# Softmax sums added later, rotations and weight halves taken earlier, and tiles handed over two behind between two layers of a hybrid attention kernel

## The chip, the cores and the metric

One NeuronCore of a Trainium2 chip runs the whole kernel. The metric is the device time of one execution in microseconds (us), the median over the runs. PE is TensorE, ACT ScalarE, DVE VectorE, POOL GpSimd, SP SyncE, which here only issues transfers.

## The reference

Two layers run over 512 latent and 256 context tokens of width 1024. Each has three groups of heads that share one input and one output projection; the last layer needs no context output:

```python
h = layer_norm(x) * (1 + sc) + sh                 # sh, sc, gt from silu(c) @ w_ada + b_ada
gq, gk, gv, dq, dk, dv, mq, mkv, mkr, ga, gb, gc = split(h @ w_in)
o_a = attention(rope(rms(gq)), rope(rms(gk)), gv)            # grouped queries, 6 heads of 64
o_b = rms(attention(q1, k1, dv) - lam * attention(q2, k2, dv))   # differential, 4 heads, q/k of 32
o_c = attention([q_nope, rope(q_pe)], [k_nope, rope(k_pe)], v)   # latent, 6 heads of 64 + 32
y = concat(o_a*silu(ga), o_b*silu(gb), o_c*silu(gc)) @ w_out
x = layer_norm(alpha * x + gt * y) * ln_g + ln_b
```

## The kernel before

Everything is float32. A weight or an activation is split into a rounded half ("high", ACT) and the rest ("low", DVE or POOL), and three matmuls make one product (lines 931 to 933, `three`). The order of every engine is written out by hand, one block per engine, and semaphores tie them together; nothing is scheduled by a tool. `L` is 0 for the first and 1 for the last layer.

**Attention** (`attend` on each engine) goes over ten pairs of maps, p = 0 to 9. Pairs 0, 1, 5 and 6 are differential (one matmul per block of scores), 2 to 4 grouped (two), 7 to 9 latent (three). For pair p PE does these things, and in between the same for its neighbours:

- `max_tile(L, p + 1, i)`, i = 0 to 7 (8 in layer 0): 96 or 128 rows of scores of a coming pair, two banks each, in two places by turns. DVE takes the row maximum (`reduce_max`, L2066), and only then may the tile after the next use the banks.
- `scores(L, p, step)` (L1166), into a ring of three banks; ACT exponentiates each (`exponent`, L1533). A bank is free for the third use behind it when ACT has read it. `RING` lists that order.
- `mix(L, p, step)` (L1182, L1188): probabilities times values, two maps side by side, each 64 columns wide. The "ctx" step is that of the context's own queries, layer 0 only.
- `denominators(L, p)` (L1207, L1210): 32 columns wide. They need the sum of the six exponentiated blocks of a map: POOL adds four of them (`sum_probs`, L1839), DVE the last (`sum_last`, L2092). ACT copies them out (`copy_denominators`), PE turns them (L1218) and the output (L1200), each into the ring.

The latent pairs' operands are made on the way: `mla_head` on PE, `mla_copy` and `mla_high` on ACT (L1425), `mla_rope` (L2074 to L2076) and `mla_low` (L2083, L2085) on DVE. The queries and keys of pairs 5 and 6 are split in `split_block(L, "diff1")` (ACT, then POOL, L1844 and L1847), and SP moves them into place in `load_unit`, with a row of ones for each map.

**Between the layers** PE does the second half of the output projection tile by tile (`project_out`, order 2, 3, 4, 5, 0, 1). DVE adds the residual and normalises a tile (`new_row`), POOL takes the root, ACT writes the next layer's normalised row (`next_row`), PE transposes it (`turn_x`, L965), ACT modulates it (`modulate_next`, L1695), and DVE splits it (`split_next`, L2248, L2249). `LAG = 3` says that tile n - 3 is transposed behind tile n's projection. The next layer's first projection begins with weight slices 0 to 2 for the first two tiles, and then takes slices 3 to 5, which are called HELD: they lie in a place that is free only when the output projection is done, and ACT and POOL split them there.

## Time and profile before

| | |
|---|---|
| time, median of 3 runs | 991.64 us (990.2 to 991.74) |
| the profiled execution's own time | 989.4 us |
| its span | 987.6 us |
| PE busy | 926.8 us (94%) |
| DVE, POOL, ACT busy | 556.1, 509.2, 426.3 us |
| PE waits for DVE's maxima (L1141) | 12.6 us in 10 waits |

A share of busy time says which engine is full, not what a change is worth: for that one looks at what PE waits for and where. Of PE's 61 us of idle time, 21 lie in the first 50 us and 11 in the last 38.

### The profile page before, as it was taken

What the parts mean: (1) busy time and instruction counts of PE and PEld (TensorE: products, weight loads), DVE (VectorE), ACT (ScalarE), POOL (GpSimd) and SP (SyncE); (2) the same over time, 40 slices, a digit from 0 to 9 for tenths busy, and PEclk for the clock granted to TensorE, in tenths of its full rate; (3) what the DMA queues carried; (4) which work ended last, traced back from release to release, by engine and by line L of the source; (5) the groups of instructions that cost most, each with busy time, mean ns of one, the idle gap of its engine ahead of it and who ended that gap; (6) DMA issues with size and microseconds to landing.
All of it is one profiled execution on the core that took longest, in us unless ns stands there. A gap on an engine that the chain in (4) does not pass through costs nothing.

```text
span 987.6 us, 13216 instructions
## 1 busy us (share of the span) xinstructions
PE 926.8 (94%) x4607; PEld 660.9 (67%) x4607; DVE 556.1 (56%) x873; ACT 426.3 (43%) x873; POOL 509.2 (52%) x433
## 2 busy tenths in 40 slices
PE   4799999999989999999999799999997999999996
PEld 1378867789746665666678589888973555565675
DVE  4426525333577569972318847567256757983236
ACT  1512212423546556655334952234343545564432
POOL 2125523324478635566546527455446865566671
PEclk9699999999999999999999999999998999999998
DMA  9955454213522310010253202323351130020242
GB/s 359 333 187 191 146 192 145 64 43 83 139 60 49 82 32 18 17 65 1 98 186 129 94 16 77 93 69 96 79 131 35 33 81 17 17 71 10 99 159 86
DMA packets 44690, 95.88 MB, mean 97 GB/s; under 512 B 9560, under 2 KB 16624, under 8 KB 42576
## 3 DMA queue, kind: packets, MB, share of 16 engines
q1 hardware_dynamic: 44624, 95.03, 31.1%
q8 instruction: 38, 0.62, 0.3%
q14 instruction: 28, 0.23, 0.1%
HBM read 71.33 MB, written 4.21 MB: 76 GB/s over the span
## 4 chain that ended last, share of the span: by engine, by line
PE 79%; DVE 5%; POOL 4%; ACT 4%; issue 3%; DMA 3%; SPq 2%; ACTq 0%; POOLq 0%; DVEq 0%
PE banks L931 15%; PE banks L933 14%; PE banks L932 14%; PE banks L1166 11%; PE banks L1188 10%; PE banks L1141 5%; PE banks L942 2%; DMA area_g<-in_w_ada_dram 2%; PE banks L1207 1%; PE banks L1200 1%; POOL w_split L1791 1%; POOL w_raw L1839 1%; PE banks L1039 1%; DVE area_b L2218 1%; PE banks L1303 1%
## 5 line engine op out<-in xcount | busy, mean ns | idle before, releaser
L1791 POOL TENSOR_TENSOR w_split<-w_raw,w_split 128x512 fp32r<-128x512 f32 (+4 forms) x121 | 147.3, 1226 | 226.5 <-ACT w_split L1425 226.5
L931 PE MATMUL banks<-w_split,area_a 128*128 128x512 f32 (+3 forms) x606 | 230.9, 381 | 10.6 <-DVE area_a L2249 6.8
L933 PE MATMUL banks<-w_split,area_a 128*128 128x512 f32 (+3 forms) x606 | 223.5, 369 | 0.0
L932 PE MATMUL banks<-w_split,area_a 128*128 128x512 f32 (+3 forms) x606 | 223.2, 368 | 0.0
L2066 DVE TENSOR_REDUCE negmax<-banks 128x1 f32<-128x768 f32 x160 | 150.3, 952 | 71.6 <-PE banks L1141 71.2
L1425 ACT ACTIVATE w_split<-w_raw 128x512 fp32r<-128x512 f32 (+4 forms) x121 | 68.4, 580 | 203.4 <-PE banks L933 197.7
L1533 ACT ACTIVATE area_z<-banks 128x512 f32<-128x512 f32 x196 | 108.6, 597 | 84.1 <-PE banks L1166 81.1
L931 PEld LDWEIGHTS banks<-w_split,area_a 128*128 128x128 f32 x606 | 115.1, 190 | 42.1 <-issue 19.8
L1166 PE MATMUL banks<-area_a 97*128 97x512 f32 (+4 forms) x448 | 130.3, 402 | 4.4 <-ACT area_z L1533 3.2
L933 PEld LDWEIGHTS banks<-w_split,area_a 128*128 128x128 f32 x606 | 115.0, 190 | 16.7
L932 PEld LDWEIGHTS banks<-w_split,area_a 128*128 128x128 f32 x606 | 115.4, 190 | 13.0
L1166 PEld LDWEIGHTS banks<-area_a 97*128 97x128 f32 (+2 forms) x448 | 78.1, 192 | 57.4 <-issue 24.3
L1141 PE MATMUL banks<-area_a 96*128 96x384 f32 (+1 forms) x288 | 78.4, 361 | 15.1 <-DVE negmax L2066 12.6
L1188 PE MATMUL banks<-area_z,vals 128*64 128x512 f32 x360 | 91.4, 612 | 0.0
L1839 POOL TENSOR_TENSOR area_b<-area_b,area_z 128x512 f32<-128x512 f32 x56 | 73.9, 1342 | 19.1 <-ACT area_z L1533 19.1
L1141 PEld LDWEIGHTS banks<-area_a 96*128 96x128 f32 (+1 forms) x288 | 50.6, 194 | 43.1 <-issue 34.8
L2039 DVE COPY area_b<-banks 128x512 f32<-128x512 f32 (+1 forms) x27 | 15.7, 583 | 69.1 <-PE banks L1039 69.1
L1425 ACT ACTIVATE area_b<-banks 128x512 f32<-128x512 f32 (+4 forms) x66 | 32.1, 509 | 47.7 <-PE banks L933 24.4
L1820 POOL TENSOR_TENSOR area_g<-area_g,o_v 128x768 f32<-128x768 f32 (+3 forms) x20 | 26.4, 1319 | 49.7 <-DVE o_v L2118 33.6
L1839 POOL TENSOR_TENSOR w_raw<-w_raw,area_z 128x512 f32<-128x512 f32 x38 | 47.5, 1276 | 7.3 <-ACT area_z L1533 7.3
L1796 POOL TENSOR_TENSOR rstd<-var,half 128x8 f32<-128x8 f32 (+2 forms) x30 | 35.4, 1189 | 20.5 <-DVE var L1945 20.5
L1533 ACT ACTIVATE late_bias<-banks 128x512 f32<-128x512 f32 x64 | 35.5, 596 | 23.3 <-PE banks L1166 22.4
(204 smaller groups left out, 1438.6 us busy)
## 6 DMA issues: line engine op xcount, KB each, us to landing
area_g<-in_w_ada_dram SPq DMA_DIRECT2D x16, 1024.0 KB, 5.5
w_raw<-in_w_in_dram SPq DMA_DIRECT2D x32, 512.0 KB, 3.6
area_g<-in_w_ada_dram SPq DMA_DIRECT2D x16, 512.0 KB, 4.9
w_raw<-in_w_out_dram SPq DMA_DIRECT2D x16, 512.0 KB, 4.5
area_a<-parts SPq DMA_DIRECT2D x72, 96.0 KB
area_a<-parts SPq DMA_DIRECT2D x30, 192.0 KB, 3.6
area_b<-in_x_dram SPq DMA_DIRECT2D x8, 512.0 KB, 9.3
w_raw<-in_w_in_dram SPq DMA_DIRECT2D x8, 352.0 KB, 3.9
```

Source lines behind the costliest of these rows:

```text
L931: nc.tensor.matmul(dst, a[0], b[0], start=first, stop=False)
L932: nc.tensor.matmul(dst, a[0], b[1], start=False, stop=False)
L933: return nc.tensor.matmul(dst, a[1], b[0], start=False, stop=last)
L1141: mm = nc.tensor.matmul(banks[:, b0 + j, 0:384], f[0][0:rows, t * P:(t + 1) * P], f[2][0:rows, j * 384:(j + 1) * 384], start=True, stop=True)
L1166: mm = nc.tensor.matmul(dst[:, at:at + cols.stop - cols.start], f[kf][0:rows, kt * P:(kt + 1) * P], f[qf][0:rows, cols], start=(i == 0), s ...
L1188: mm = nc.tensor.matmul(banks[64 * u:64 * u + 64, 3, :], vals[:, step, value_head(2 * p + u), :], prob(L, p, step, u), start=(step == 0), ...
L1425: return nc.scalar.activation(dst, src, ACT.Copy)
L1533: nc.scalar.activation(prob(L, p, step, u), banks[:, r % NRING, :], ACT.Exp, scale=SCALE[pair_family(p)]).then_inc(p_ready, 1)
L1791: op = nc.gpsimd.tensor_tensor(lo, raw, hi.bitcast(F32), ALU.subtract)
L1796: nc.gpsimd.tensor_tensor(rstd[:, cols], var[:, cols], half[:, cols], ALU.pow).then_inc(root_ready, 1)
L1839: nc.gpsimd.tensor_tensor(total(L, p, u), first, prob(L, p, step, u), ALU.add).then_inc(pool_summed, 1)
L2066: nc.vector.tensor_reduce(negmax[:, p % 2, at:at + 1], banks[:, b0:b0 + 2, 0:384], AX.XY, ALU.max, negate=True).then_inc(max_read, 1)
```

## The change

It moves instructions on PE, ACT, DVE and SP, takes five small transfers per layer away, and moves one split from POOL to DVE. Counts of the arithmetic stay as they are. The diff is cut: first the tables, then SP's loads, PE's `attend` and `project_out`, ACT's `attend` and DVE's `attend`.

```diff
-LAG = 3
+LAG = 2
...
-        return (2, 4, 6, 0, 6, 0)[out_tiles(L - 1).index(use[2])] + use[3]
+        return (2, 4, 6, 4, 0, 6)[out_tiles(L - 1).index(use[2])] + use[3]
...
-LOADS = {"gqa": 3, "diff": 7, "mla": 3}
+ONES = (12, 13, 14)
+def loads(u):
+    own = u < 4 or u in (16, 19)
+    return {"gqa": 3, "diff": 6, "mla": 2}[family(u)] + int(own)
...
+                for b in ONES:
+                    slab_used(sp, L, b - KD)
+                    load_one(blocks[96:97, b, :], ones_in)
...
                     if context:
+                        scores(L, p, 2)
+                        max_tile(L, p + 1, 8)
                         mix(L, p - 1, "ctx")
+                        denominators(L, p - 1)
                     else:
                         mix(L, p - 1, 4)
                         mix(L, p - 1, 5)
-                    scores(L, p, 2)
-                    max_tile(L, p + 1, 8)
-                    denominators(L, p - 1)
+                        denominators(L, p - 1)
+                        scores(L, p, 2)
                     scores(L, p, 3)
...
+                    both = out_tiles(L)[:2] if L == DEPTH - 1 and n == 0 else [t]
...
                     for k in range(KD):
                         pe.wait_ge(w_lo, N_SLICE["out", L, 1, k])
-                        mm = three(bank(use), [h_t[:, i, k, t * P:(t + 1) * P] for i in range(2)],
-                                   late_slice(k), k == 0, k == KD - 1)
+                        for o in both:
+                            mm = three(bank(("y", L, 1, o)), [h_t[:, i, k, o * P:(o + 1) * P] for i in range(2)],
+                                       late_slice(k), k == 0, k == KD - 1)
...
-                    if head_pair(p + 2):
-                        mla_high(L, 2 * p + 4)
                     exponent(L, p, 1)
                     if context:
+                        exponent(L, p, 2)
                         copy_context(L, p - 1)
+                        copy_denominators(L, p - 1)
                     else:
                         copy_latents(L, p - 1)
+                        copy_denominators(L, p - 1)
+                        exponent(L, p, 2)
                     if head_pair(p + 2):
                         mla_high(L, 2 * p + 5)
-                    exponent(L, p, 2)
-                    copy_denominators(L, p - 1)
                     exponent(L, p, 3)
...
+                    if p == 2:
+                        split_block(L, "diff1")
...
                     if context:
                         exponent(L, p, "ctx")
+                    if head_pair(p + 3):
+                        mla_high(L, 2 * p + 6)
...
                 for i in range(EARLY):
                     reduce_max(L, 2, i)
-                    if i in (2, 3):
-                        sum_last(L, 0, i - 2)
...
                     reduce_max(L, p + 1, 6)
-                    if head_pair(p + 2):
-                        mla_low(L, 2 * p + 4)
+                    sum_last(L, p - 1, 0)
+                    sum_last(L, p - 1, 1)
                     reduce_max(L, p + 1, 7)
...
                     reduce_max(L, p + 2, 1)
+                    if head_pair(p + 3):
+                        mla_rope(L, 2 * p + 6)
+                    if p == 2:
+                        split_last(L)
                     reduce_max(L, p + 2, 2)
                     reduce_max(L, p + 2, 3)
                     if head_pair(p + 3):
-                        mla_rope(L, 2 * p + 6)
-                    if p < NPAIR:
-                        sum_last(L, p, 0)
+                        mla_rope(L, 2 * p + 7)
                     reduce_max(L, p + 2, 4)
-                    if p < NPAIR:
-                        sum_last(L, p, 1)
                     reduce_max(L, p + 2, 5)
                     if diff:
                         diff_norm(L, p - 1)
                     if head_pair(p + 3):
-                        mla_rope(L, 2 * p + 7)
+                        mla_low(L, 2 * p + 6)
```

`RING` is rewritten to match. `last_pair` is changed in the same way. `split_last` is the low half of "diff1", as two tensor_tensor on DVE, taken off POOL. In the last layer DVE keeps two tiles in work: `gained_tile` of the next tile stands ahead of `new_row` of tiles 0 and 2. ACT calls `next_row` ahead of `modulate_next` for every tile.

**DVE at the start of attention, last layer.** L2066 (L2090 in the changed file) is the row maximum of a tile; the first two and the last of pair 1 and those of pair 2 stand here. L2092 (L2125) is the last addition of pair 0, into `w_raw`. Before:

```order
L2066 TENSOR_REDUCE negmax<-banks 128x1 [waits filled,max_filled]
L2066 TENSOR_REDUCE negmax<-banks 128x1 [waits max_filled] x2
L2092 TENSOR_TENSOR w_raw<-w_raw,late_bias 128x512 [waits p_ready,pool_summed]
L2066 TENSOR_REDUCE negmax<-banks 128x1 [waits max_filled]
L2092 TENSOR_TENSOR w_raw<-w_raw,late_bias 128x512 [waits p_ready,pool_summed]
L2066 TENSOR_REDUCE negmax<-banks 128x1 [waits max_filled] x4
L2106 RECIPROCAL rec<-banks 128x8 [waits ring_filled]
```

The same place of the changed kernel:

```order
L2090 TENSOR_REDUCE negmax<-banks 128x1 [waits filled,max_filled]
L2090 TENSOR_REDUCE negmax<-banks 128x1 [waits max_filled] x6
L2125 TENSOR_TENSOR w_raw<-w_raw,late_bias 128x512 [waits p_ready,pool_summed] x2
L2090 TENSOR_REDUCE negmax<-banks 128x1 [waits max_filled]
L2139 RECIPROCAL rec<-banks 128x8 [waits ring_filled]
```

Both additions moved behind four more maxima, with one left behind them.

**PE in pair 5, last layer.** From the last `mix` of pair 4 (L1188, L1198 in the changed file) over the denominators (L1207, L1217), scores 2 and 3 of pair 5 (L1166, L1176) and a maximum tile of pair 7 (L1141, L1151) to the transposed output (L1200, L1210). Before:

```order
L1188 MATMUL banks<-late_bias,vals 64x512
L1166 MATMUL banks<-area_a 128x512 [waits p_ready] x2
L1207 MATMUL banks<-area_b,ones_c 32x512 [waits p_ready,dve_summed]
L1207 MATMUL banks<-area_b,ones_c 32x512
L1166 MATMUL banks<-area_a 128x512 [waits p_ready] x2
L1141 MATMUL banks<-area_a 128x384 [waits max_read,mla_lo,unit_in14]
L1141 MATMUL banks<-area_a 128x384
L1218 MATMUL banks<-ident,scr 128x64 [waits d_copied]
L1218 MATMUL banks<-ident,scr 128x64 x3
L1200 MATMUL banks<-ident,o_t 128x128 [waits p_ready,o_copied]
```

The same place of the changed kernel:

```order
L1198 MATMUL banks<-late_bias,vals 64x512
L1217 MATMUL banks<-area_b,ones_c 32x512 [waits p_ready,dve_summed]
L1217 MATMUL banks<-area_b,ones_c 32x512
L1176 MATMUL banks<-area_a 128x512 [waits p_ready] x2
L1176 MATMUL banks<-area_a 128x512 [waits d_copied]
L1176 MATMUL banks<-area_a 128x512 [waits p_ready]
L1151 MATMUL banks<-area_a 128x384 [waits mla_lo,max_read,ones_in,unit_in14]
L1151 MATMUL banks<-area_a 128x384
L1228 MATMUL banks<-ident,scr 128x64 [waits p_ready,d_copied]
L1228 MATMUL banks<-ident,scr 128x64 x3
L1210 MATMUL banks<-ident,o_t 128x128 [waits p_ready,o_copied]
```

The denominators moved ahead of scores 2, and one bank of scores 3 now waits for their copy (`d_copied`).

**ACT at the same place.** L1533 (L1554) are exponentials, L1425 (L1446) copies: `area_a<-area_b` is `mla_high`, `o_t` the output of pair 4, `scr` its denominators. Before:

```order
L1425 ACTIVATE area_b<-banks 64x256 [waits ring_filled]
L1533 ACTIVATE area_z<-banks 128x512 [waits pool_summed,p_used,ring_filled] x2
L1425 ACTIVATE area_a<-area_b 96x512 [waits ring_filled,mla_roped]
L1425 ACTIVATE area_a<-area_b 64x768
L1533 ACTIVATE area_z<-banks 128x512 [waits pool_summed,p_used,ring_filled] x2
L1425 ACTIVATE o_t<-banks 128x512 [waits p_used,ring_filled]
L1425 ACTIVATE area_a<-area_b 96x512 [waits ring_filled,mla_roped]
L1425 ACTIVATE area_a<-area_b 64x768
L1533 ACTIVATE area_z<-banks 128x512 [waits pool_summed,p_used,ring_filled] x2
L1425 ACTIVATE scr<-banks 64x512 [waits ring_filled,rec_done]
L1533 ACTIVATE late_bias<-banks 128x512 [waits dve_summed,p_used,ring_filled] x2
```

The same place of the changed kernel:

```order
L1446 ACTIVATE area_b<-banks 64x256 [waits ring_filled]
L1446 ACTIVATE area_a<-area_b 96x512 [waits ring_filled,mla_roped]
L1446 ACTIVATE area_a<-area_b 64x768
L1554 ACTIVATE area_z<-banks 128x512 [waits pool_summed,p_used,ring_filled] x4
L1446 ACTIVATE o_t<-banks 128x512 [waits p_used,ring_filled]
L1446 ACTIVATE scr<-banks 64x512 [waits ring_filled,rec_done]
L1554 ACTIVATE area_z<-banks 128x512 [waits pool_summed,p_used,ring_filled] x2
L1446 ACTIVATE area_a<-area_b 96x512 [waits ring_filled,mla_roped]
L1446 ACTIVATE area_a<-area_b 64x768
L1554 ACTIVATE late_bias<-banks 128x512 [waits dve_summed,p_used,ring_filled] x2
```

One `mla_high` moved ahead of the pair's first exponential, the other from between exponentials 1 and 2 to between 2 and 3.

## Rows read from the trace of the kernel before

**Rows 1.** The page, part 1: busy time, share of the span, instructions.

```profile
PE 926.8 (94%) x4607; PEld 660.9 (67%) x4607; DVE 556.1 (56%) x873; ACT 426.3 (43%) x873; POOL 509.2 (52%) x433
```

**Rows 2.** PE's waits: for whom, us in total, times, longest.

```profile
PE banks L1141 <- DVE negmax L2066: 12.6, 10, 5.2
...
PE banks L1141 <- DMA area_a<-ones_r: 1.0, 2, 0.6
```

**Rows 3.** Timeline, attention's start, layer 0: start, duration, instruction [idle before].

```profile
278.25 1.81 POOL L1844 TENSOR_TENSOR parts<-area_b,parts 128x768 fp32r<-128x768 f32 x1
...
277.11 3.51 DVE L2092 TENSOR_TENSOR w_raw<-w_raw,area_z 128x512 f32<-128x512 f32 x1 [0.98 <-POOL w_raw L1839]
...
281.63 0.98 PE L1141 MATMUL banks<-area_a 128*128 128x384 f32 x2 [3.42 <-DVE negmax L2066]
```

**Rows 4.** Timeline, the same place in the last layer, and pair 2's.

```profile
746.53 2.96 DVE L2092 TENSOR_TENSOR w_raw<-w_raw,late_bias 128x512 f32<-128x512 f32 x1 [1.93 <-POOL w_raw L1839]
...
747.66 1.28 POOL L1844 TENSOR_TENSOR parts<-area_b,parts 128x512 fp32r<-128x512 f32 x1
...
750.50 0.98 PE L1141 MATMUL banks<-area_a 128*128 128x384 f32 x2 [5.17 <-DVE negmax L2066]
...
771.28 0.59 PE L1141 MATMUL banks<-area_a 128*128 128x384 f32 x2 [0.93 <-DVE negmax L2066]
```

**Rows 5.** Stretches: busy time of PE, PEld, DVE, ACT, POOL, PE's clock, DMA.

```profile
568.00:571.40 3.40, 3.40 (x8) 2.68 (x9) 2.83 (x4) 1.07 (x3) 1.71 (x2) 0.50 0.14 17
750.50:755.90 5.40, 5.40 (x14) 3.46 (x16) 4.11 (x5) 2.17 (x4) 1.70 (x2) 0.50 0.58 134
772.00:778.00 6.00, 6.00 (x29) 2.85 (x26) 1.41 (x3) 3.36 (x6) 5.63 (x6) 1.00 0.41 94
```

**Rows 6.** Timeline, narrow steps between wide ones.

```profile
445.43 0.40 PE L1135 MATMUL banks<-cmp_t 96*128 96x256 f32 x2
...
445.76 0.62 PE L1207 MATMUL banks<-area_b,ones_c 128*32 128x512 f32 x2
...
446.21 0.60 PE L1207 MATMUL banks<-area_b,ones_c 128*32 128x512 f32 x2
...
446.75 0.97 PE L1166 MATMUL banks<-parts 97*128 97x512 f32 x3
```

**Rows 7.** Timeline, pair 5 of the last layer.

```profile
832.45 1.05 PE L1207 MATMUL banks<-area_b,ones_c 128*32 128x512 f32 x4
834.34 0.98 PE L1166 MATMUL banks<-area_a 97*128 97x512 f32 x2 [0.84 <-ACT area_z L1533]
...
836.00 0.66 PE L1200 MATMUL banks<-ident,o_t 128*128 128x128 f32 x4
...
828.39 1.35 ACT L1425 ACTIVATE area_a<-area_b 96x512 fp32r<-96x512 f32 x2
829.65 1.06 ACT L1533 ACTIVATE area_z<-banks 128x512 f32<-128x512 f32 x2
...
830.37 3.12 POOL L1839 TENSOR_TENSOR area_b<-area_z 128x512 f32<-128x512 f32 x2 [7.37 <-ACT area_z L1533]
```

**Rows 8.** Timeline, the same stretch, DVE.

```profile
827.70 0.68 DVE L2092 TENSOR_TENSOR area_b<-area_b,late_bias 128x512 f32<-128x512 f32 x1
828.30 0.95 DVE L2066 TENSOR_REDUCE negmax<-banks 128x1 f32<-128x768 f32 x1
...
833.97 0.94 DVE L2085 TENSOR_TENSOR area_a<-area_b,area_a 64x768 fp32r<-64x768 f32 x1
```

**Rows 9.** Timeline, between the layers.

```profile
567.84 0.80 PE L931 MATMUL banks<-w_split,area_a 128*128 128x512 f32 x1 [6.80 <-DVE area_a L2249]
...
568.43 1.28 POOL L1791 TENSOR_TENSOR cmp_t<-w_raw,cmp_t 128x512 fp32r<-128x512 f32 x1
```

**Rows 10.** Timeline, end of the program.

```profile
957.33 0.50 PE L931 MATMUL banks<-cmp_t,area_a 128*128 128x512 f32 x1 [0.57 <-POOL cmp_t L1791]
...
983.23 1.28 DVE L2235 SCALAR_TENSOR_TENSOR area_b<-o_t,row_std,area_g 128x1024 f32<-128x1024 f32 x1 [0.97 <-POOL row_std L1804]
```

126 lines of the change are left out of this document (78 added, 48 removed).

## The prediction, made blind

> **What bounds the kernel now.** I read the page, then the waits of PE, then the timeline of all engines where PE waits. PE is busy for 94% of the span [rows 1], so a change that leaves PE's work as it is can give back only what PE waits for, and what it does at the lower of its two clocks. The waits view puts 12.6 us on DVE's row maxima, in ten waits [rows 2]; two of them are most of it. At the start of attention PE is idle for 3.42 us in layer 0 [rows 3] and for 5.17 us in the last layer [rows 4], because DVE stands at `sum_last` and the maxima are queued behind it. Behind that idle time, and behind the 6.80 us between the layers [rows 9], the granted clock is 0.50, that is 1.2 GHz, for 3.4 to 5.4 us; in a stretch without such a wait before it it is 1.00 [rows 5].
>
> The other waits are small and stand at fixed places: in the differential pairs next to the latent ones (5 and 6), where ACT has `mla_high` between the exponentials [rows 7], and at the weights of the last projection [rows 10]. The sum is made against the profiled execution, 989.4 us, which is 2.2 us below the median of the runs, 991.64.
>
> **Attention's start, layer 0.** The DVE add of 277.11 took 3.51 us for what takes 0.68 elsewhere [rows 3, 8]: it ended 0.56 us behind POOL's split, which ran from 278.25 to 280.06. The changed DVE does maxima 3, 4, 5 and 6 of pair 2 first. Max 3's scores were there at 276.5, so the tile that started at 281.63 can start at 277.95. From there I put durations in PE's new order: scores 0 at 278.3, max 6 at 278.8, scores 1 until 279.9, scores 2 until 281.5 (its second bank waits for an exponential), max 8 until 281.95, context mix until 282.95. The two adds now stand behind max 6 on DVE (280.8) and meet POOL's first sum of pair 1, so they end at 283.4 and the denominators start at 283.45. Before, the same set of instructions ended with denominators at 287.4. Gain 4.0 us, the lower clock's part included.
>
> **The same, last layer.** Max 3 can be read at 744.6, so the tile of 750.50 starts at 745.6. Scores 0, max 6, scores 1, max 7 and the two mixes bring PE to 749.75. The denominators now follow at once, and their adds are late: POOL is at sums until 747.7 and at the split until 748.94 [rows 4], then one add, one POOL sum (1.26), one add: 751.4. Denominators until 752.45 and scores 2 until 752.95; scores 3 begin there against 758.65 before, less some 0.3 for the bank that waits for `d_copied`. Gain 5.2 us. Bounds: 3.9 if both of POOL's queued operations pass first, as in the 2.96 us of 746.53 [rows 4], 6.5 if the adds wait for nobody.
>
> **The pairs after it.** The adds no longer stand between maxima 3, 4 and 5. That removes PE's 0.93 us at 771.28 [rows 4] and two of its kind (0.62 at 789.1, 0.3 at 764.7), all three read off the same view as the ten waits of [rows 2]: 1.9 us. Against it, in the last layer's grouped pairs the adds come some 0.2 us later than the mixes end: two matmuls per bank give 4.7 us from scores 0 to the denominators, and DVE needs 4.9 (maximum 6 until 2.35, add, one POOL sum, add). Three pairs, 0.6 us. Net -1.3.
>
> **Rows of ones and "diff1".** PE waits twice for a row of ones, 1.0 us in total [rows 2], 1.3 with the restart. The split is taken before scores 4 of pair 2 instead of behind them, its low half goes to DVE, which then stands without its adds there, and each load has one transfer less. DVE's two subtractions (0.7 and 0.9 [rows 8]) hold up maximum 2, whose successor on PE is due over 2 us later: nothing. Gain 1.3; without that cover a loss of 1.6 per layer.
>
> **Narrow steps side by side.** A 256-column matmul goes out every 0.12 us, but the 32-column one follows the last (445.55) after 0.21: 0.09 to enter [rows 6]. Inside, the pace is 0.45 (445.76 to 446.21), and the wide one comes 0.54 later (446.75): 0.09 to leave. The change removes one leaving and one entering in each of 18 places. No row has 64 columns directly followed by 32. Its cost lies between nothing and one of these 0.09, so a place gives 0.09 to 0.18; I take 0.1, since both kinds of entry cost the same here. In seven places the adds are late anyway (below) and nothing is gained: 11 x 0.1 = 1.1 us. The Trainium skill, TensorEngine Tiling (Array Packing), Key Properties, says that changing the tiling mode, not just the tile, drains the engine; by it 64 to 32 is such a change, which leaves one of two and is the lower value. The trace has no such pair to confirm it.
>
> **Pairs 5 and 6: a loss.** These have one matmul per bank, so PE is fast and ACT and DVE are late. Last layer, pair 5, from scores 0 at 826.99: `mla_low` now stands between maxima 5 and 6. Max 5 ends at 828.65, `mla_low` (0.6 + 0.94 [rows 8]) at 830.1, max 6 (0.9) at 831.0. POOL's two sums of pair 5 begin at 829.3, when the exponential is there, and the add waits for the second: 831.8, so the adds end at 832.4 and 833.1. PE is at the denominators at 831.0 and waits 2.1 us. Then denominators until 834.05, copy on ACT until 834.75, exponential 2 until 835.8, `mla_high` (1.35 [rows 7]) until 837.1, first half of exponential 3 at 837.7. The transposed output needs that bank, in the ring of three: 837.8 instead of 836.00 [rows 7]. Loss 1.8 us, although the old wait of 0.84 at 834.34 is gone. Layer 0 gives the same sum (add ready 1.6 us behind the context mix, output at 376.1 instead of 374.4): 1.7. Two pairs in each layer: +7.0. Bounds: if the adds wait for nobody and DVE is early, the output comes at 835.7, -0.3 each and -1 in all; if each add loses one more POOL sum, +12. I take the chain. Pair 7 of the last layer has the same `mla_low` and a `diff_norm` ahead of max 6, with 5.4 us on PE until the denominators and 7 on DVE: +1.3. Pair 7 of layer 0 has the context's steps as cover.
>
> The Trainium skill, SBUF — State Buffer, Who interferes with whom, calls the pair of ports that DVE and GpSimd share an exclusive lock, for DVE operations with two SBUF inputs too, where the first to issue blocks the other for its whole length. The trace agrees (3.51 against 0.68 us), and it speaks against this change, which puts adds where POOL's sums begin.
>
> **Between the layers.** Before, PE waits from 561.0 for tile 3's split, 6.80 us [rows 9], then runs 3.8 us at the lower clock. With tiles two behind, ACT has per tile two squares (1.34 each), a row (1.25) and a modulation (2.9): 6.8 us, more than PE's 6.3, so PE waits 1.1 and 1.0 us for the first and fourth row. Slices 0 to 2 of tiles 2 and 3 then run from 561.5 to 565.6 unhindered. But now the HELD slices are due: POOL's last split, 568.43 to 569.7 [rows 9] with PE not waiting for it, comes at 570.5 to 571.8, because ACT's second square stands behind the HELD high halves and later than before. PE waits 6.2 us for that and runs on slowly. Slices 6 and 7 begin at 591.9 instead of 591.2: +0.7. What is late next is the weights, no longer the rows. Bounds -3 (the split at 568) and +3.
>
> **The end.** The first tile of the last projection takes 8.9 us instead of 5.5, since its slices 4 to 7 come one each 1.3 to 1.7 us [rows 10]. Two tiles by turns need 1.37 us per slice, so nothing waits: both are done at 964.84, the last tile at 975.8 instead of 979.25. DVE has 4.35 us per tile, four tiles from 964.2, and ends at 981.7 instead of 984.5 [rows 10]. -2.8, bounds -3.4 and -1.5 (two stores back to back).
>
> **Sum.** -4.0 - 5.2 - 1.3 - 1.3 - 1.1 + 7.0 + 1.3 + 0.7 - 2.8 = -6.7 us: 982.7 on the profiled execution's scale, 984.9 on the median's; I say 984.5.
>
> **Rivals.** *The adds are in time* (0.27). DVE reaches them before POOL's first sum, or gets the ports between two sums. For it: POOL is idle for 7.37 us ahead of 830.37 [rows 7]. Against it: DVE's own queue ends at 831.0. Then pairs 5 to 7 give -1 instead of +8.3, and the sum is about -16: 975.5. *The boundary gives what it was laid out for* (0.10): the HELD slices are split by 567 and PE's wait is gone, 6.2 us and the slow clock: 977. *No change* (0.04): the new waits take all of it, because the ring and not the adds bounds pairs 1 to 4 too: 990. *Slower* (0.07): every add waits for one more POOL sum, 1.26 us, in all 18 places. The forecast gain is used up at 0.37 us a pair; at 0.7 (half hidden) it is 12.6 - 6.7, or 997.5. For it: both long adds [rows 3, 4] let two POOL operations pass. Against it: in most pairs POOL has one operation in flight.
>
> **How the numbers follow.** My case has 0.52, with a range of its own of 981 to 989. The range 974 to 989.5 takes in the first two rivals and leaves out the others, about 2 in 10 with the edges. A measurement of this kernel tells from about 0.2%, or 2 us. Faster by more: 0.52 + 0.27 + 0.10, less a little at the upper edge, 0.88; within it 0.05; slower 0.07.
>
> **What would show it.** Right: no idle before the sixth tile of pair 2; the adds of pairs 5 and 6 over 1.2 us each, with PE's wait in front of the denominators put on DVE's add; a wait for ACT ahead of the transposed output; a wait for `cmp_t` from POOL between the layers; no wait in the last projection. Wrong: no wait at the denominators of pairs 5 and 6 (then 975), or one at nearly all pairs (then slower).

## The result: 0.7% slower

The changed kernel takes 998.34 us (median of 4 runs, 997.83 to 998.81), the kernel before 990.92 us on the same chips (4 runs, 989.47 to 991.74): ratio 1.0074, 95% interval 1.0059 to 1.009. The prediction was 984.5 us, with 989.5 as its upper end. The profiled execution took 998.17 us with a span of 996.4 us, 8.8 us more than the span before.

The page, part 1, of the changed kernel:

```profile
PE 929.0 (93%) x4607; PEld 660.9 (66%) x4607; DVE 567.4 (57%) x877; ACT 427.8 (43%) x873; POOL 510.9 (51%) x429
```

DVE is busy 11 us longer than in [rows 1]. The four subtractions of "diff1" that it took over are 4.8 of them; the rest is the same arithmetic, taking longer. PE's waits (for whom, us in total, times, longest):

```profile
PE banks L1151 <- DVE negmax L2090: 7.0, 9, 2.1
PE banks L1217 <- DVE area_b L2125: 6.1, 6, 3.0
PE banks L944 <- POOL cmp_t L1815: 5.6, 1, 5.6
PE banks L1217 <- DVE w_raw L2125: 4.4, 5, 2.8
PE banks L1210 <- ACT area_z L1554: 4.1, 4, 1.3
...
PE banks L1210 <- ACT late_bias L1554: 1.4, 2, 1.1
```

The long waits for maxima of [rows 2] are gone, 12.6 us became 7.0. In their place stand 10.5 us at the denominators (L1217), in eleven waits for DVE's last additions (L2125), and 5.5 us at the transposed output (L1210).

To find the place, I compared the start of the same ACT exponential in both timelines; their order is the same in both kernels.

| exponential | before, us | after, us | difference | gained or lost since the row above |
|---|---|---|---|---|
| layer 0, pair 0, first | 262.58 | 262.56 | -0.02 | |
| pair 1, first | 283.08 | 278.78 | -4.30 | -4.3 |
| pair 5, first | 366.57 | 362.44 | -4.13 | +0.2 |
| pair 7, first | 416.96 | 415.06 | -1.90 | +2.2 |
| pair 8, first | 439.98 | 439.01 | -0.97 | +0.9 |
| pair 9, fourth | 469.31 | 467.95 | -1.36 | -0.4 |
| last layer, pair 0, first | 731.97 | 732.63 | +0.66 | +2.0 |
| pair 1, fourth | 759.32 | 755.91 | -3.41 | -4.1 |
| pair 5, first | 827.42 | 821.66 | -5.76 | -2.4 |
| pair 7, first | 871.25 | 876.30 | +5.05 | **+10.8** |
| pair 8, first | 890.97 | 902.27 | +11.30 | **+6.2** |
| pair 9, fourth | 917.02 | 927.77 | +10.75 | -0.6 |
| end of the span | 987.6 | 996.4 | +8.8 | -2.0 |

So the change did most of what it was to do, and 17 us were lost in three pairs, 5 to 7 of the last layer. The timeline of DVE, PE and POOL in pair 5 there (start, duration, instruction, idle before):

```profile
820.13 0.69 DVE L2098 TENSOR_TENSOR scr<-area_b,rt 32x512 f32<-32x512 f32 x1
...
821.55 0.68 DVE L2100 TENSOR_TENSOR area_b<-area_b,scr 32x512 f32<-32x512 f32 x1
...
822.27 1.82 DVE L2090 TENSOR_REDUCE negmax<-banks 128x1 f32<-128x768 f32 x2
823.37 0.58 PE L1151 MATMUL banks<-area_a 96*128 96x384 f32 x2 [1.51 <-DVE negmax L2090]
...
824.73 0.94 DVE L2109 TENSOR_TENSOR area_a<-area_b,area_a 64x768 fp32r<-64x768 f32 x1
824.96 3.52 POOL L1863 TENSOR_TENSOR area_b<-area_z 128x512 f32<-128x512 f32 x2 [7.26 <-ACT area_z L1554]
...
826.46 2.56 DVE L2125 TENSOR_TENSOR area_b<-area_b,late_bias 128x512 f32<-128x512 f32 x2
...
829.08 1.05 PE L1217 MATMUL banks<-area_b,ones_c 128*32 128x512 f32 x4 [0.85 <-DVE area_b L2125]
...
833.67 0.63 PE L1210 MATMUL banks<-ident,o_t 128*128 128x128 f32 x4 [1.07 <-ACT late_bias L1554]
```

`mla_rope` (2.1 us) now stands ahead of maximum 4, and PE waits 1.51 us for that maximum. Then come `mla_low`, maximum 6, and the additions, which meet POOL's first sums: 2.56 us for two, where two alone take 1.4 [rows 8]. Pairs 6 and 7 repeat it with waits of 2.08 and 1.13 us for the maximum and 0.84 and 3.04 us at the denominators (the expectation of e9 below puts the last in pair 6; it stands in pair 7). None of this came singly: behind the waits the granted clock falls. Stretches of the changed kernel (busy time of PE, PEld, DVE, ACT, POOL, PE's clock, DMA):

```profile
819.00:822.00 3.00, 2.86 (x14) 1.30 (x10) 2.92 (x5) 1.75 (x4) 0.00 (x0) 1.00 0.12 28
...
824.30:827.70 3.40, 3.40 (x11) 1.21 (x10) 3.40 (x5) 1.00 (x2) 2.74 (x2) 0.53 0.00 0
...
834.50:837.90 3.40, 3.40 (x11) 0.77 (x8) 3.40 (x4) 0.27 (x1) 2.70 (x2) 0.53 0.03 6
...
885.70:889.10 3.40, 3.40 (x9) 1.64 (x6) 0.46 (x1) 0.91 (x2) 0.00 (x0) 0.53 0.00 0
```

There are five such rows between 824 and 890 (two more from 851.6 and from 861.8), 17.0 us in which PE is busy without a gap at a mean clock of 0.53, that is mostly at 1.2 GHz. At full clock the same work takes 17.0 x 0.53, so they cost 8.0 us. The kernel before had no such stretch in these pairs. The rest is PE's waits, 11.9 us there against 3.1: with the 8.0 this makes 16.8 of the 17.1 us.

### The profile page after: what moved, and what is told of

It is laid out like the page before. It is cut to its first block, busy times and chain, and to the rows that moved or that the text cites. A ratio compares the mean times of both kernels' runs of the same rounds, so it can differ in the third digit from the quotient of the medians.

```text
span 996.4 us, 13272 instructions
## 1 busy us (share of the span) xinstructions
PE 929.0 (93%) x4607; PEld 660.9 (66%) x4607; DVE 567.4 (57%) x877; ACT 427.8 (43%) x873; POOL 510.9 (51%) x429
## 4 chain that ended last, share of the span: by engine, by line
PE 72%; DVE 15%; ACT 4%; DMA 3%; POOL 3%; issue 2%; SPq 1%; POOLq 0%; ACTq 0%; DVEq 0%
PE banks L944 14%; PE banks L946 13%; PE banks L945 13%; PE banks L1176 9%; PE banks L1198 8%; DVE negmax L2090 4%; PE banks L1151 4%; PE banks L955 2%; PE banks L1217 2%; DMA area_g<-in_w_ada_dram 2%; DVE area_b L2125 2%; DVE w_raw L2125 1%; PE banks L1210 1%; DVE area_b L2099 1%; DVE area_b L2100 1%
## 5 line engine op out<-in xcount | busy, mean ns | idle before, releaser
L2090 DVE TENSOR_REDUCE negmax<-banks 128x1 f32<-128x768 f32 x160 | 148.4, 950 | 62.2 <-PE banks L1151 61.8
L1446 ACT ACTIVATE w_split<-w_raw 128x512 fp32r<-128x512 f32 (+4 forms) x121 | 68.3, 580 | 204.6 <-PE banks L946 198.9
L1554 ACT ACTIVATE area_z<-banks 128x512 f32<-128x512 f32 x196 | 109.1, 599 | 83.4 <-PE banks L1176 72.8
L1176 PE MATMUL banks<-area_a 97*128 97x512 f32 (+4 forms) x448 | 128.0, 399 | 1.2 <-ACT late_bias L1554 0.4
L1176 PEld LDWEIGHTS banks<-area_a 97*128 97x128 f32 (+2 forms) x448 | 78.0, 190 | 47.5 <-issue 23.7
L1198 PE MATMUL banks<-area_z,vals 128*64 128x512 f32 x360 | 94.9, 632 | 0.0
L1151 PE MATMUL banks<-area_a 96*128 96x384 f32 (+1 forms) x288 | 77.1, 356 | 8.5 <-DVE negmax L2090 7.0
L1151 PEld LDWEIGHTS banks<-area_a 96*128 96x128 f32 (+1 forms) x288 | 49.8, 190 | 35.0 <-issue 28.2
L2063 DVE COPY area_b<-banks 128x512 f32<-128x512 f32 (+1 forms) x27 | 15.7, 583 | 69.1 <-PE banks L1049 69.1
L1863 POOL TENSOR_TENSOR w_raw<-w_raw,area_z 128x512 f32<-128x512 f32 x38 | 49.6, 1331 | 8.8 <-ACT area_z L1554 8.6
L1446 ACT ACTIVATE area_b<-banks 128x512 f32<-128x512 f32 (+4 forms) x66 | 32.0, 508 | 50.1 <-PE banks L946 23.8
L1554 ACT ACTIVATE late_bias<-banks 128x512 f32<-128x512 f32 x64 | 35.7, 599 | 22.7 <-PE banks L1176 18.2
```

What stands on the lines that cost most here:

```text
L1151: mm = nc.tensor.matmul(banks[:, b0 + j, 0:384], f[0][0:rows, t * P:(t + 1) * P], f[2][0:rows, j * 384:(j + 1) * 384], start=True, stop=True)
L1176: mm = nc.tensor.matmul(dst[:, at:at + cols.stop - cols.start], f[kf][0:rows, kt * P:(kt + 1) * P], f[qf][0:rows, cols], start=(i == 0), s ...
L1198: mm = nc.tensor.matmul(banks[64 * u:64 * u + 64, 3, :], vals[:, step, value_head(2 * p + u), :], prob(L, p, step, u), start=(step == 0), ...
L1446: return nc.scalar.activation(dst, src, ACT.Copy)
L1554: nc.scalar.activation(prob(L, p, step, u), banks[:, r % NRING, :], ACT.Exp, scale=SCALE[pair_family(p)]).then_inc(p_ready, 1)
L1863: nc.gpsimd.tensor_tensor(total(L, p, u), first, prob(L, p, step, u), ALU.add).then_inc(pool_summed, 1)
```

## Experiments

Fifteen kernels, by the question that each answers. "Both back" means the changed kernel with adds and rotations at their old places. Results first; ratios are to the kernel before on the same chip.

| run | median, us | ratio (95% interval) |
|---|---|---|
| e1: DVE's ropes back | 1009.32 | 1.0177 (1.0154 to 1.02) |
| e2: ropes, `mla_low`, `mla_high` back | 1004.26 | 1.0128 (1.0107 to 1.0149) |
| e3: adds of pairs 1 to 9 back | 1000.51 | 1.0084 (1.006 to 1.0108) |
| e4: both back | 986.25 | 0.9947 (0.9929 to 0.9966) |
| e5: e4, layer 0's second `mla_high` of a pair behind exponential 2 | 984.88 | 0.9962 (0.9939 to 0.9985) |
| e6: e5, between the layers as before | 986.89 | 0.996 (0.9945 to 0.9975) |
| e7: e4, denominators behind scores 2 | 984.84 | 0.9947 (0.9927 to 0.9967) |
| e8: before, only the end changed | 990.33 | 0.9993 (0.998 to 1.0005) |
| e9: changed, POOL waits for the adds | 985.08 | 0.994 (0.9919 to 0.9962) |
| e10: combined | 979.96 | 0.989 (0.9872 to 0.9908) |
| e11: combined, POOL waits in pair 1 | 972.11 | 0.9809 (0.9791 to 0.9826) |
| e12: before, only pair 0's adds late | 983.41 | 0.9922 (0.9894 to 0.9951) |
| e13: e2 and POOL waits | 998.09 | 1.0062 (1.0042 to 1.0082) |
| e14: e3 and POOL waits | 990.91 | 0.9993 (0.9973 to 1.0014) |
| e15: e11 with two tiles behind | 976.33 | 0.9832 (0.9809 to 0.9855) |

### Adds or rotations? e1 to e4

e1, on DVE:

```diff
-                    if head_pair(p + 3):
-                        mla_rope(L, 2 * p + 6)
                     reduce_max(L, p + 2, 2)
                     reduce_max(L, p + 2, 3)
                     if head_pair(p + 3):
-                        mla_rope(L, 2 * p + 7)
+                        mla_rope(L, 2 * p + 6)
                     reduce_max(L, p + 2, 4)
                     reduce_max(L, p + 2, 5)
                     if diff:
                         diff_norm(L, p - 1)
+                    if head_pair(p + 3):
+                        mla_rope(L, 2 * p + 7)
```

> Theory R (rotations): in the changed kernel DVE has a whole mla_rope (2.1 us) ahead of maximum 4, so it is late at the maxima of the latent pairs; in pairs 5 to 7 of the last layer PE waits 4.7 us in three waits for them, and the granted clock is 0.53 for 3.4 us behind each. Only the two mla_rope go back to their old places here. R expects these 4.7 us and three of the five slow stretches (1.7 us each) gone: 998.3 - 9.8 = 988.5 us. Theory A (adds): the loss comes from the last additions, which wait for POOL behind maximum 6; the ropes are not what is late. A expects 996 to 998.5 us, with the 4.7 us turned into waits for the adds.

1009.32 us: neither theory. The waits for maxima on L1151 fell from 7.0 to 2.9 us, and the adds became later still: 15.7 us in four waits at the denominators, the longest 5.2. The second rope now stands behind maximum 5 and ahead of `mla_low`, maximum 6 and the adds: in pair 5 of the last layer DVE goes without a pause from that rope (829.68) to the adds (836.07), and PE waits 5.15 us for them.

e2 puts `mla_low` behind maximum 6 and both `mla_high` behind exponentials 0 and 1 as well.

> As the run before, but mla_low on DVE and mla_high on ACT go back too, so that only the adds and the order of the narrow steps stay changed in attention. R expects 986 to 989 us (the old 0.84 us wait for an exponential behind mla_high comes back, the ones at the transposed output go). A expects 995 to 998 us and the waits at the denominators of pairs 5 and 6 unchanged at 0.9 us or more each.

1004.26 us, 16.5 us in six waits at the denominators. The adds now stand behind maximum 6 and `mla_low`.

e3, the adds:

```diff
                     reduce_max(L, p + 1, 6)
-                    sum_last(L, p - 1, 0)
-                    sum_last(L, p - 1, 1)
+                    if p == 1:
+                        sum_last(L, 0, 0)
+                        sum_last(L, 0, 1)
...
+                    sum_last(L, p, 0)
                     reduce_max(L, p + 2, 4)
+                    sum_last(L, p, 1)
                     reduce_max(L, p + 2, 5)
```

> The changed kernel with the last additions of pairs 1 to 9 back between maxima 3, 4 and 5; pair 0's stay where the change puts them, and the rotations stay changed. A expects the 10.5 us of PE's 11 waits at the denominators gone and two slow stretches of 1.7 us with them: 984.5 us. R expects only the waits outside pairs 5 to 7 gone, since DVE is late at the maxima there all the more: 998.3 - 4.5 = 993.8 us, or worse.

1000.51 us (nine runs from 992.95 to 1003.6, the widest scatter of all). The waits for the adds in pairs 1 to 9 are gone, and PE waits 9.4 us in eleven waits for maxima: adds and ropes stand ahead of them. Pairs 5 to 7 of the last layer lose 17.0 us, as much as in the changed kernel.

> Adds of pairs 1 to 9 and all rotation steps back; changed remain the start of attention, the narrow steps side by side, the ones and diff1, the boundary and the end. By the trace of the two kernels attention lost 3.2 us in pairs 5 to 7 of layer 0 and 17.1 in the last layer, both of which should be gone: 998.3 - 20.3 = 978 us, if R and A between them are the whole loss. If a third thing (denominators directly behind the value steps, with their bank and copy) holds part of it, 982 to 988 us, with PE waiting for ACT's copies in pairs 5 to 7.

e4 holds both edits and takes 986.25 us. Against it the adds' move alone costs 18.0 us (e2), the rotations' alone 14.3 (e3), and the two together 12.1 (the changed kernel). So the costs do not add: they are one queue, DVE's, between maximum 3 and the denominators. The time lies in the expectation's other range, that of a third cause. By the profile (982.76 us, the lowest of six runs) pairs 5 to 7 still lose 3.9 us in layer 0, where PE waits 1.82 us twice for an exponential behind `mla_high`, and 1.8 in the last layer.

### The order of the denominators, the boundary, the end: e5 to e8

```diff
 # e5, ACT, layer 0 only
-                    if head_pair(p + 2):
-                        mla_high(L, 2 * p + 5)
                     if context:
                         exponent(L, p, 2)
                         copy_context(L, p - 1)
                         copy_denominators(L, p - 1)
+                    if head_pair(p + 2):
+                        mla_high(L, 2 * p + 5)
```

> The last kernel (both back, 986.25 us) with one more edit: in layer 0 the second mla_high of a pair stands behind exponential 2, not between 1 and 2. There PE waits 1.82 us twice for an exponential behind mla_high (pairs 5 and 6 of layer 0), and the trace shows a stretch at clock 0.53 behind each. Theory 'the copy on ACT's queue is the whole of what is left in these pairs': 3.6 us of waits and two times 1.7 us of slow clock go, 986.25 - 7 = 979 us. Rival 'the ring only hands the wait on to the transposed output', as in the changed kernel (3 waits of about 1.1 us): 984 to 986 us.

984.88 us, not told from e4 by the intervals. In layer 0, pairs 5 to 7 lose 5.8 us against before (first exponentials of pairs 5 and 8), where e4 lost 3.9. The time is the rival's, but the trace speaks for neither theory, because the edit moved the wrong copy. Both waits of 1.82 us are still there:

```profile
363.15 1.57 ACT L1446 ACTIVATE area_a<-area_b 96x768 fp32r<-96x768 f32 x2
...
365.25 0.54 PE L1176 MATMUL banks<-area_a 97*128 97x512 f32 x1 [1.82 <-ACT area_z L1554]
```

PE waits here for exponential 1, which stands behind the pair's first `mla_high`, and that one e5 leaves in its place. New are waits of 1.31 us twice and 0.43 us once for the transposed output, whose bank waits for exponential 3 behind the copy that was moved.

e6 is e5 with `LAG = 3`, the old bank map, PE's old first slices and ACT's old order.

> The kernel of the run before with the part between the layers put back (LAG = 3, bank map, order of first slices, ACT's order of row and modulation). The milestones put the next layer's first exponential 2.0 us later against the last one of layer 0 in the changed kernel than before, and 3.7 us in the kernel with both back. If two tiles behind is a loss of its own (HELD slices split late), this run is 2.0 to 3.7 us faster than the one before it. If the difference is only where the slow stretch falls against PE's idle time, it is within 1 us of it either way. The prediction's term would make it 0.7 us faster.

986.89 us, unclear: the two scatter by 6 and 9 us. By the profiles, from pair 9's fourth exponential to the next layer's first, three tiles behind are 0.9 us faster. See e15.

e7 is e4 with scores 2 ahead of the denominators again, in `RING`, on PE and on ACT.

> The both-back kernel of the first four runs with the denominators behind scores 2 again (ring, PE and ACT orders of before); left of the change are pair 0's adds, ones and diff1, the boundary and the end. The prediction's term (0.1 us in 11 of 18 places, here in all 18) says 1.1 to 1.8 us slower than with them side by side, if nothing else moves; but the 1.82 us waits in layer 0 and the 0.84 us waits for the denominators' copy in the last layer belong to the order, so those (5.3 us and slow stretches of 1.7 us) go and before's 1.7 us come back. Theory 'the order itself loses': 980 to 983 us. Theory 'the order itself is worth its 1.8 us': 987 to 988 us.

984.84 us, between the two theories and the same as e4, from parts of opposite sign. In pairs 5 to 7 of layer 0 it loses 0.1 us against before, where e4 lost 3.9. In pairs 1 to 4 the side-by-side order of e4 is 0.57 us better in layer 0 and 0.54 us from pair 2 to 5 in the last layer, 0.14 and 0.18 a place. And at the start of the last layer e7 is 3.9 us worse:

```profile
745.61 1.29 POOL L1853 TENSOR_TENSOR w_raw<-w_raw,area_z 128x512 f32<-128x512 f32 x1
746.85 1.28 POOL L1858 TENSOR_TENSOR parts<-area_b,parts 128x512 fp32r<-128x512 f32 x1
747.11 7.07 DVE L2115 TENSOR_TENSOR w_raw<-w_raw,late_bias 128x512 f32<-128x512 f32 x2
748.09 2.50 POOL L1853 TENSOR_TENSOR w_raw<-area_z 128x512 f32<-128x512 f32 x2
750.55 2.48 POOL L1853 TENSOR_TENSOR w_raw<-w_raw,area_z 128x512 f32<-128x512 f32 x2
754.24 1.07 PE L1217 MATMUL banks<-w_raw,ones_c 128*32 128x512 f32 x2 [4.59 <-DVE w_raw L2115]
```

Two additions that take 1.4 us alone took 7.07: the first 6.47, the second 0.68. POOL ran six operations without a pause from 745.61 to 753.03, five of them still to end when the first addition began, and it ended only behind the last of them. With exponential 2 ready early, POOL had two sums more to go on with.

e8 has only the end in the kernel before.

> The kernel before with only the end changed (two tiles of the last projection by turns, DVE with two tiles in work). Prediction's term: -2.8 us, 990.7 - 2.8 = 987.9. Bounds -3.4 and -1.5. Rival 'stores and the last normalisation hold the end whatever PE does': 990.7 within 0.5 us.

990.33 us against 991.05, not told from no change by its interval. By the trace the part behind pair 9's fourth exponential takes 68.65 us instead of 70.58: -1.9 us, and 68.5 to 68.7 in every profile with the changed end.

### POOL against DVE: e9, e13, e14

```diff
             def sum_probs(L, p, step):
                 for u in range(2):
+                    if step == 1 and PN[L, p] >= 1:
+                        pool.wait_ge(dve_summed, N_DVE_SUM[PAIRS[PN[L, p] - 1] + (1,)])
```

> The changed kernel with one wait more: POOL begins a pair's first sum only when DVE's last additions of the pair before are done, so the two never meet there. In the changed kernel these additions take up to 2.3 us each at the start of the last layer (two in 4.65 us, while POOL is busy without a gap), where they take 0.68 alone, and PE waits 10.5 us in 11 waits for them. Theory L (DVE's additions get nothing while POOL goes on): most of the waits at the denominators go (the 2.84 us of pair 0 in the last layer, 3.0 in pair 6), 7 to 9 us with the slow stretches: 988 to 991 us. Theory Q (DVE's own queue of mla_low, maximum 6 and the ropes is late; POOL is not the matter): only pair 0's wait goes, 995 us, and PE's waits in pairs 5 to 7 stay within 1 us of what they are.

985.08 us: one wait more on POOL made the changed kernel 13.3 us faster, more than the 7 to 9 us of theory L. At the start of the last layer, in e9:

```profile
746.09 1.26 POOL L1870 TENSOR_TENSOR parts<-area_b,parts 128x512 fp32r<-128x512 f32 x1
746.32 2.19 DVE L2127 TENSOR_TENSOR w_raw<-w_raw,late_bias 128x512 f32<-128x512 f32 x2
...
748.56 1.05 PE L1217 MATMUL banks<-w_raw,ones_c 128*32 128x512 f32 x4 [0.38 <-DVE w_raw L2127]
...
748.63 2.51 POOL L1865 TENSOR_TENSOR w_raw<-area_z 128x512 f32<-128x512 f32 x2 [1.29 <-DVE w_raw L2127]
```

The same place of the changed kernel:

```profile
748.38 1.28 POOL L1868 TENSOR_TENSOR parts<-area_b,parts 128x512 fp32r<-128x512 f32 x1
748.61 4.65 DVE L2125 TENSOR_TENSOR w_raw<-w_raw,late_bias 128x512 f32<-128x512 f32 x2
...
749.62 2.48 POOL L1863 TENSOR_TENSOR w_raw<-area_z 128x512 f32<-128x512 f32 x2
...
753.31 1.05 PE L1217 MATMUL banks<-w_raw,ones_c 128*32 128x512 f32 x4 [2.84 <-DVE w_raw L2125]
```

The additions take 2.19 us, the rest of POOL's split, and PE's wait falls from 2.84 to 0.38. In all, the denominators' waits fell from 10.5 to 1.5 us, and of the 17.0 us at the lower clock in pairs 5 to 7, 10.2 are left. The 4.7 us of waits for maxima there are unchanged, and these pairs still lose 10.1 us against before, by the first exponentials of pairs 5 and 8. e13 and e14 ask what holds that rest.

e13 is e2 with e9's wait, e14 is e3 with it.

> The changed kernel with POOL's wait and with all rotation steps (mla_rope, mla_low, mla_high) back at their old places; the adds stay behind maximum 6. With POOL's wait alone it took 985.1 us, and pairs 5 to 7 of the last layer still lost 10 us against before, with 4.7 us of PE's waits on row maxima. Theory 'the ropes' new places hold the rest': the 4.7 us and up to two slow stretches go, 977 to 980 us. Theory 'the queue in front of the adds' (mla_low, then maximum 6, then the adds; without POOL's wait this kernel's PE waited 16.5 us in six waits at the denominators): POOL's wait gives back only POOL's part, and the time is 986 to 992 us, slower than with the ropes early.

> The changed kernel with POOL's wait and the adds of pairs 1 to 9 back between maxima 3, 4 and 5; the rotations stay changed. Theory 'ropes': PE's waits on maxima in pairs 5 to 7 of the last layer (6.9 us in four waits with the adds back and no wait on POOL) stay, since the adds there were never late: 988 to 992 us. Theory L alone (POOL and DVE meeting at the adds is the whole loss): 978 to 982 us.

PE's waits in pairs 5 to 7 of the last layer, in e13 and then in e14:

```profile
PE banks L1217 <- DVE area_b L2128: 9.8, 3, 3.4
PE banks L1151 <- DVE negmax L2093: 0.8, 2, 0.4
```

```profile
PE banks L1151 <- DVE negmax L2092: 7.0, 4, 2.7
PE banks L1210 <- ACT late_bias L1554: 1.4, 2, 1.1
PE banks L1210 <- ACT area_z L1554: 1.1, 1, 1.1
```

998.09 and 990.91 us. POOL is out of the way in both, and DVE's own queue is still late: with adds behind `mla_low` and maximum 6 at the denominators (9.8 us), with ropes ahead of maximum 4 at the maxima (7.0 us). Only with both back (e4) are both kinds gone: 2.8 us of waits for maxima in the last layer, none for adds.

### The start alone and the best combination: e10 to e12, e15

e12 is the kernel before with one edit:

```diff
                 for i in range(EARLY):
                     reduce_max(L, 2, i)
-                    if i in (2, 3):
-                        sum_last(L, 0, i - 2)
...
                     reduce_max(L, p + 1, 6)
+                    if p == 1:
+                        sum_last(L, 0, 0)
+                        sum_last(L, 0, 1)
```

> The kernel before with one edit: pair 0's two additions behind maximum 6 of the first iteration instead of between the early maxima, in both layers. The prediction's terms are -4.0 in layer 0 and -5.2 in the last layer: 991 - 9.2 = 981.8 us. In the traces so far the milestones give -4.3 in layer 0 (adds hidden) and, with scores 2 ahead of the denominators as here, -5.5 + 3.9 in the last layer, because POOL goes on without a gap there and DVE's two additions took 7.07 us: 991 - 5.9 = 985.1 us. No gain at all (991) if the clock's slow stretch at both places stays.

983.41 us, -7.3 on its chip and between the two forecasts: two instructions moved give as much as the whole change was forecast to give (-6.7). The profile is that of the fastest run (980.04 us); in it the start gains 4.3 us in layer 0, up to pair 1's first exponential, and 5.9 in the last layer, up to its fourth. The order at the start of the last layer is that of e7, yet the two additions took 2.52 us there, not 7.07, and PE did not wait for them:

```profile
744.32 1.27 POOL L1844 TENSOR_TENSOR parts<-area_b,parts 128x512 fp32r<-128x512 f32 x1
745.30 2.52 DVE L2092 TENSOR_TENSOR w_raw<-w_raw,late_bias 128x512 f32<-128x512 f32 x2
...
745.62 3.34 POOL L1839 TENSOR_TENSOR w_raw<-area_z 128x512 f32<-128x512 f32 x2
```

PE was at 1.2 GHz from 742.5 to 745.9, POOL had a gap of 0.02 us behind its split, and the first addition, begun 0.3 us before the split's end (in e7 1.0 before), was done at 746.14, in the middle of POOL's next sum. So the same order gave 2.5 us in one kernel and 7.1 in the other. That the gap decides it is my reading and not shown.

e10 takes e4, with the old order of scores 2 and denominators in pairs 5 to 7 and the boundary of before:

```diff
+def side(p):
+    return not 5 <= p <= 7
...
+        if not side(_p):
+            RING += row + third + den
+        elif ctx:
+            RING += third + row + den
+        else:
+            RING += row + den + third
```

and the same case on PE and ACT. e11 adds one wait:

```diff
+                    if step == 1 and p == 1:
+                        pool.wait_ge(dve_summed, N_DVE_SUM[PAIRS[PN[L, p] - 1] + (1,)])
```

> What the runs so far speak for: pair 0's adds late, all other adds and the rotations where they were before, denominators side by side with the value steps except in pairs 5 to 7 (there the old order), ones and diff1, the boundary as before, the end as changed. Worked out against the kernel with the denominators back (984.84 us): the boundary of before 1.5 to 2 us faster at the same clock, the narrow steps 0.16 us a place in some 10 places by the milestones, and the start of the last layer 2.5 us less (its adds took 7.07 us there and 2.5 to 4.65 with denominators ahead of scores 2). Sum 984.84 - 6 = 979 us. If these pieces do not add because each moves the place of the next slow stretch: 983 to 986 us.

> The kernel of the run before, with POOL's first sum of pair 1 waiting for DVE's additions of pair 0 in both layers. Theory L: in the last layer these two additions end at 1.4 us instead of 4.65 us behind their start, and PE's wait of 2.84 us in front of the first denominators goes: 2.8 us faster than the run before, 976 us, up to 1.7 us more where a slow stretch goes too. Theory Q: no difference over 0.5 us.

979.96 us, as worked out from the pieces, and 972.11 us, 1.9% faster than the kernel before and 4 us below what theory L gave. The profile of e11 is that of its slowest run, 976.22 us, which is what theory L gave; there the start of the last layer is 2.6 us faster than in e10. The two profiles differ by 3.9 us; the rest of the 7.9 between the medians no trace shows. In e11 the two additions stand so:

```profile
744.11 1.27 POOL L1899 TENSOR_TENSOR parts<-area_b,parts 128x512 fp32r<-128x512 f32 x1
745.23 1.31 DVE L2156 TENSOR_TENSOR w_raw<-w_raw,late_bias 128x512 f32<-128x512 f32 x2
...
747.56 1.05 PE L1227 MATMUL banks<-w_raw,ones_c 128*32 128x512 f32 x4
```

No wait at all in front of the denominators (e10: 2.8 us).

> The fastest kernel so far (combined, POOL waiting in pair 1, 972.11 us) with the change's part between the layers put in. At the same place of the slow stretch the milestones make two tiles behind 1.5 to 2 us slower: 973.6 to 974.1 us, up to 1.7 us more if the stretch moves. The prediction's term of +0.7 gives 972.8; its other bound, -3 (the HELD slices split in time), 969.

976.33 us. The intervals of e15 and e11 just overlap, but the profiles agree: from pair 9's fourth exponential to the next layer's first it takes 262.7 to 264.4 us in six profiles with three tiles behind (mean 263.6) and 264.5 to 266.3 in eleven with two (mean 265.3). The two pairs of kernels that differ in nothing else give less: 0.9 us (e5, e6) and 0.7 (e15, e11).

## Why the prediction was wrong, step by step

**The step that failed: "Pairs 5 and 6: a loss", +7.0, with pair 7's +1.3.** For the last layer it gave 3.6 for two pairs and 1.3 for the third; they cost 10.8 and 6.2. In both layers these pairs cost 20.2 us instead of 8.3, and that is 11.9 of the 15.5 us between the forecast of -6.7 and the 8.8 of the profile.

In layer 0 the size was near, 3.4 forecast and 2.2 measured for pairs 5 and 6 (and 0.9 in pair 7, where nothing was forecast), but that was in part luck. PE waited 0.47 and 0.46 us for the adds there, not 1.6. e3, whose adds are not late in these pairs, loses as much, and e7, which has the old order of scores 2 and denominators, loses 0.1. So most of the loss in layer 0 goes with that order and its ring, the last link of the step's chain: PE waited 1.31 us twice for the transposed output. The changed kernel with the old order alone was not run.

For the last layer three things were left out.

1. *The rope ahead of maximum 4.* The step put only `mla_low` into DVE's queue ("Max 5 ends at 828.65"), though `mla_rope` had moved ahead of maximum 4 in the same diff. The 4.7 us of waits for maxima come from there: with the ropes back (e1, e2, e13) 0.8 us is left of them, and e3 and e14, which move the ropes and not the adds, have 6.9 and 7.0.
2. *The clock.* The prediction noted that long waits are followed by 1.2 GHz [rows 5], and priced no such stretch for the waits it forecast. It forecast waits of 1.6 and 2.1 us at the denominators; those that came, 0.84 to 3.04 us there and 1.13 to 2.08 at the maxima, had five stretches and 8.0 us behind them.
3. *POOL.* "The add waits for the second" sum was the right mechanism and too small: two adds took 2.56 us in pairs 5 and 6 and 3.21 in pair 7. Keeping POOL back gave 7 us in pairs 5 to 7 of the last layer (17.1 lost becomes 10.1) and 13.3 in all (e9).

The **slower rival** (0.07) had the mechanism of the adds, with waits in all 18 places, and its 997.5 us is near the 998.34 measured. That is luck: PE waited for the adds in eleven places, 10.5 us in all, and the loss sat in three pairs, where ropes, adds and clock came together. The Trainium skill (SBUF — State Buffer, Who interferes with whom) calls the ports that DVE and GpSimd share an exclusive lock. The trace of e7 agrees, and shows a wait over more than one operation: an addition took 6.47 us against 0.68, behind five operations of POOL. The prediction cited the rule against the change and then priced it at one sum per add. Of the other rivals, *the adds are in time* fails by the same waits, and *the boundary gives what it was laid out for* by the 5.58 us that PE waits for the HELD slices.

**Start, layer 0**, -4.0: measured -4.3, by the mechanism given. The adds met POOL's first sums, and PE waited 0.34 us:

```profile
280.81 2.37 DVE L2125 TENSOR_TENSOR w_raw<-w_raw,area_z 128x512 f32<-128x512 f32 x2
280.99 3.32 POOL L1863 TENSOR_TENSOR w_raw<-late_bias,area_z 128x512 f32<-128x512 f32 x2 [0.89 <-ACT area_z L1554]
...
283.23 0.62 PE L1217 MATMUL banks<-w_raw,ones_c 128*32 128x512 f32 x2 [0.34 <-DVE w_raw L2125]
```

**Start, last layer**, -5.2: -5.5 at pair 1's first exponential, and 1.4 given back at its denominators, -4.1. Near the lower bound of 3.9, for the reason named there: POOL's queued operations passed first. e11, where PE does not wait for these adds, gains 5.6 us up to pair 1's fourth exponential, where the changed kernel has the 4.1.

**Later maxima** -1.3: wrong in cause and sign. The waits of 0.93 and 0.62 us are gone in e3, e4 and e7 as well, where these adds stand between maxima 3, 4 and 5 as before. They are still there in e12 (0.93 and 0.64), which has "diff1" and the ones at their old places. The third wait of the term, 0.3 us at 764.7, is 0.03 in the trace and none of the ten. What the adds' new place does is seen between e3 and the changed kernel: from pair 2's first exponential to pair 5's first, 55.78 us become 56.66 in the last layer, and 65.20 become 65.35 in layer 0. PE went from the last 64-column step to the first 32-column one in 1.17, 1.09 and 0.76 us in pairs 1 to 3 of the last layer, where 0.52 is the pace without a wait (e10). So the late adds cost 1.5 us at the denominators where 0.6 was forecast, and what they give back is 0.6, not 1.9.

**Ones and diff1** -1.3: twice the size forecast, and all of it in the last layer. Over the same stretch e7, whose adds and narrow steps stand as before there, takes 65.78 us in layer 0, as before, and 56.29 in the last layer instead of 58.88. The two waits for rows of ones are gone: between pair 3's fourth exponential and pair 4's first the changed kernel gained 0.6 us in layer 0 and 0.9 in the last layer. But in layer 0 DVE's two subtractions took 0.94 and 2.04 us, and PE waited 0.26 and 0.28 us for maxima behind them, for which the term had nothing.

**Narrow steps** -1.1 at 0.1 a place: measured 0.14 to 0.18 a place (e4 against e7), near the other bound. From 64 to 32 columns, pair 8 of layer 0:

```profile
443.59 1.08 PE L1192 MATMUL banks<-late_bias,vals 128*64 128x256 f32 x8
444.60 0.62 PE L1217 MATMUL banks<-area_b,ones_c 128*32 128x512 f32 x2
...
445.05 0.60 PE L1217 MATMUL banks<-area_b,ones_c 128*32 128x512 f32 x2
...
445.60 0.97 PE L1176 MATMUL banks<-parts 97*128 97x512 f32 x3
```

The last value step begins at 444.29 and the first of 32 columns 0.31 later; two 256-column passes take 0.21 at 2.4 GHz, which leaves 0.09 for the change of width, as for the others [rows 6]. By the Trainium skill, TensorEngine Tiling (Array Packing), Key Properties, a change of tiling mode drains the engine. The trace fits, with 0.09 us here too; that it is a drain, no trace shows. What the term left out is the ring: in pairs 5 to 7 of layer 0 the same order costs 3.8 us (e4 against e7).

**Between the layers** +0.7: measured +2.0, within its bounds. The mechanism was as forecast:

```profile
569.81 1.26 POOL L1815 TENSOR_TENSOR cmp_t<-w_raw,cmp_t 128x512 fp32r<-128x512 f32 x1
...
571.13 0.80 PE L944 MATMUL banks<-cmp_t,area_a 128*128 128x512 f32 x1 [5.58 <-POOL cmp_t L1815]
```

PE waits 5.58 us (6.2 forecast) for the HELD slices' split instead of 6.80 for the rows [rows 9]. Over all profiles two tiles behind cost 1.7 us, and 0.7 and 0.9 in the two pairs of kernels that differ in nothing else.

**The end** -2.8: measured -2.0. PE ended 2.8 us earlier against pair 9's fourth exponential (3.4 forecast); DVE then has two `new_row` back to back, 1.7 us apart, and ends 6 us behind PE instead of 5 [rows 10]:

```profile
990.31 1.28 DVE L2280 SCALAR_TENSOR_TENSOR area_b<-vals,row_std,area_g 128x1024 f32<-128x1024 f32 x1
...
992.04 1.28 DVE L2280 SCALAR_TENSOR_TENSOR area_b<-vals,row_std,area_g 128x1024 f32<-128x1024 f32 x1 [0.43 <-POOL row_std L1828]
```

## What to carry to other kernels

When a change moves several things on one engine's queue, write down that queue between the two points that PE reads, for the fullest pair, with every instruction in it: here the sum of adds, ropes and maxima mattered, and undoing one of the moves alone made it worse. An addition with two SBUF inputs on DVE wants to stand where POOL pauses; where it can't, let POOL wait for it: here that gave 13.3 us (e9) and 7.9 us (e11) by the medians. When one edit is taken back, look in the trace whether it touched the wait that it was aimed at: e5's did not. Price a new wait of a microsecond on PE with the slow stretch that may follow it, and compare such kernels by the same milestones in their timelines before believing a difference of 2 or 3 us in their medians.
